# A two-block model kernel: a spectral transform folded in half, and another order of work around the convolution after it

## The chip, the cores and the metric

The kernel runs on one core of a Trainium2 chip (eight cores, two dies of four). The metric is device time in microseconds of one execution, here the median of three. The core's engines work at once and meet through semaphores: TensorE (PE; PEld is its weight load), VectorE (DVE), ScalarE (ACT), GpSimd (POOL), and SyncE (SP), whose queue issues nearly all transfers.

## The reference, cut to what matters

A sequence of 256 rows of 1024 values goes through two blocks. The first has a recurrent mixer and an attention layer. The second begins with the part that is changed:

```
p = rmsnorm(x) @ w_in_ab                      # 1024 -> 512 (a), 512 (v), 512 (gate)
f = real(fft2(a as [256, 4 heads, 128], axes=(time, 128), ortho))
ya = einsum("bshd,hde->bshe", f, fnet_map)    # a 128x128 map per head
u = v * sigmoid(gate)
u = depthwise_conv(u, conv_w, 31 taps) + conv_b
yb = silu(layernorm(u as [4 heads, 128]))
x = x + concat(ya, yb) @ w_out_ab
...
x = x + swiglu_ffn(rmsnorm(x))                # then a pool mixer and a second FFN
```

## The kernel before, in words

**Layout.** Values lie channel by channel on the 128 partitions and the 256 time steps along the free axis, eight tiles of 128 channels.

**Weights.** Large weight matrices come as 1 MB slabs of 128x2048 values. SP loads them into a ring of five buffers (`raw`), in the order of the table `PLAN`. ACT copies each into the first half of one of four buffers `W` (line 635, the high part), and DVE writes what is left, raw minus high, into the second half (line 1030, the low part). A product takes three fast matmuls (lines 1602 to 1604: high by high, high by low, low by high). `stream(MATS[n])` emits the split of all slabs up to n at that place of an engine's program, and `fill(k)` is `stream(MATS[k + 3])`. Where the text says slab n, it is `MATS[n]`.

**Who waits.** Each engine runs its own program in the order in which it is written. PE's results go to eight banks of PSUM. The class `Outputs` gives each result its bank in turn, and before PE writes a bank it waits (`bank_free`) until the result that was there before has been read. `o.n += 4` skips four banks.

**Keys and values (first block, 120 to 165 us).** PE makes eight key tiles k0 to k7, then four value tiles v0 to v3 (128x512 each), then the queries q0 to q7, which need the low parts of their input (DVE, `r<-t,r`). ACT finishes each key with the copy of line 759, and its bank is free after that. Before, v0 takes the bank of k4.

**The spectral part (slabs 24 and 25, then 281 to 294 us).** All of it is plain fp32. Per head h, line 1891 multiplies the a-tile with a table of 128 cosines and 128 sines (`cdsd`, 128x256) for both halves of time; ACT copies and scales the eight results. Lines 1899 and 1900 sum over time with tables in `acc[0]` (128x256 each, 16 matmuls). ACT copies f, line 1906 applies `fnet_map`, ACT makes the high part of that and DVE the low part.

**The convolution of 31 taps.** Channels 0 to 2 run on DVE: `taps` is a list of 93 pairs (channel, tap), three of which (tap 0) ACT does, so DVE has 90 steps of 128x256 (line 1033, `f<-f,vec`). A step adds to its own channel's tile. The last eight of the list belong to channel 2 alone. `pump(n)` emits the next n pairs of the list. Channel 3 runs on PE (line 1913): 31 matmuls with diagonal matrices that ACT makes (`dg`, `diagonals`), eight buffers.

**The layer norm and the output product.** For a channel tile d: `ln_mean` (PE, line 1919), `ln_centre` (DVE), square (ACT), `ln_var` (PE, 1924), root (ACT), `ln_inverse` (DVE, line 1451, `lnr<-lnr`), `ln_row` (PE, line 1667, spreads the inverse over a bank), `ln_scale` (DVE), silu and high part (ACT), `ln_low` (DVE). Channel 3 goes first. PE fills the time between with `mixed(kt, c)`, products with slabs 26 to 29 (`w_out_ab`); `both(kt)` is four of these, twelve matmuls 128x512. kt 0 to 3 take the spectral part, kt 4 to 7 the convolution's. The FFN stages follow and are not touched.

Of the kernel before, what the change touches and what calls it, by code (L numbers as in the profile page):

```python
# [6 lines left out]
P, T, D, KT = 128, 256, 1024, 8  # L7
# [10 lines left out]
def slab_plan():  # L18
# [59 lines left out]
    ("norm_mix_g_2", 16), ("norm_ffn_g_2", 16), ("conv_w_2", 124), ("conv_b_2", 4), ("conv_ln_g_2", 4),  # L78
    ("conv_ln_b_2", 4), ("eps", 2),
]  # L80
# [5 lines left out]
NV = _at  # L86
CSTS = [("ident", 128), ("mask", 384), ("cdsd", 256), ("fmap", 512)]
COFF = {}
# [79 lines left out]
def outputs():  # L168
# [41 lines left out]
    o.n += 1  # L210
    o.n += 4
    for c in range(2):
# [122 lines left out]
def two_block_program(nc, w_d, vec_d, cst_d, dft_d, rcnt_d, row_d, x_d, out_d):  # L335
# [6 lines left out]
    with ctx:  # L342
# [3 lines left out]
        def sem(name):  # L346
            return ctx.enter_context(nc.semaphore(name))
# [3 lines left out]
        with ExitStack() as early:  # L351
# [66 lines left out]
        s_b, s_gpad, s_col, s_gt, s_sg, s_tap0, s_tap, s_a, s_ac, s_f, s_fhi, s_flo = (  # L418
            sem(f"s_{n}") for n in ("b", "gpad", "col", "gt", "sg", "tap0", "tap", "a", "ac", "f", "fhi", "flo"))
        s_dg, s_dgm, s_cv3, s_lnm, s_lnv, s_lnc, s_lnq, s_lnr, s_lni, s_lnb, s_lnn, s_cs2, s_clo = (  # L420
            sem(f"s_{n}") for n in ("dg", "dgm", "cv3", "lnm", "lnv", "lnc", "lnq", "lnr", "lni", "lnb", "lnn", "cs2",
# [16 lines left out]
        F0f = F0[:, 0:2048].rearrange("p (k n) -> p k n", k=8)  # L438
        PADW = T + 30
        G0 = F0[:, 0:4 * PADW].rearrange("p (k n) -> p k n", k=4)  # L440
        Vt = F2[:, :, :].rearrange("p (a b) n -> p a (b n)", a=2)
# [177 lines left out]
        @block.gpsimd  # L619
        def _(e):  # L620
            e.wait_ge(s_mv, 12)
            e.dma_start(acc[0][:, :], dft_d).then_inc(s_dft, 16)
            e.wait_ge(s_flo, 4)
            e.dma_start(rc, rcnt_d).then_inc(s_rc, 16)
            e.dma_start(prow[:, :], row_d[0]).then_inc(s_prow, 16)
            e.wait_ge(s_cv3, 1)
            e.dma_start(frow[:, :], row_d[1]).then_inc(s_frow, 16)

        @block.scalar
        def _(e):  # L630
# [249 lines left out]
            p.wait_ge(s_cst, 16)  # L880
            for c in range(2):
                fill(24 + c)
                for d in (2 * c, 2 * c + 1):
# [3 lines left out]
            for h in range(4):  # L887
                for a in range(2):
                    p.wait_ge(*ended("ac", h, a))
                    copy(AC[:, h, a, :], out_of("ac", h, a), scale=rcol[:, 4 + a:5 + a]).then_inc(s_ac, 1)  # L890
# [24 lines left out]

            diagonals(*range(6, 16))
            fill(25)
            diagonals(*range(16, 31))
# [106 lines left out]
        def _(e):  # L1025
# [417 lines left out]
            fill(25)  # L1443

# [29 lines left out]
            fill(26)  # L1474
            for d in range(3):
# [117 lines left out]
        def _(e):  # L1593
# [291 lines left out]
            for c in range(2):  # L1885
                single(24 + c, run("a", 2 * c, 2 * c + 1), R2, s_rlo, 0)
            for h in range(4):
                for a in range(2):
                    bank_free("ac", h, a)
                    p.wait_ge(s_a, h + 1)  # L1890
                    e.matmul(out_of("ac", h, a), F2[:, h, a * P:(a + 1) * P], C("cdsd"), start=True,  # L1891
                             stop=True).then_inc(s_ps, 1)
            p.wait_ge(s_dft, 16)
            for h in range(4):
                bank_free("f", h)
                out = out_of("f", h)
                for a in range(2):
                    p.wait_ge(s_ac, 2 * h + a + 1)
                    e.matmul(out, AC[:, h, a, 0:P], acc[0][:, a * T:a * T + T], start=a == 0, stop=False)
                    done = e.matmul(out, AC[:, h, a, P:256], acc[0][:, (2 + a) * T:(3 + a) * T], start=False,  # L1900
                                    stop=a == 1)
                done.then_inc(s_ps, 1)
            for h in range(4):
                bank_free("fm", h)
                p.wait_ge(s_f, h + 1)
                e.matmul(out_of("fm", h), C("fmap", h * P, P), F2[:, 4 + h, :], start=True,
                         stop=True).then_inc(s_ps, 1)
# [185 lines left out]
def constants():  # L2093

    out = np.zeros((P, NC), np.float32)

    def put(name, a):
        out[:, COFF[name]:COFF[name] + a.shape[1]] = a

    put("ident", np.eye(P))  # L2100
    diag = np.where(np.arange(P)[None, :] <= np.arange(P)[:, None], 0.0, -1e30)
    put("mask", np.concatenate([diag, np.zeros((P, P)), diag], 1))
    d = np.arange(P)
    ang = 2 * np.pi * ((d[:, None] * d[None, :]) % P) / P
    put("cdsd", np.concatenate([np.cos(ang), np.sin(ang)], 1) / np.sqrt(P))
# [76 lines left out]
```

## Time and profile before

| | before |
|---|---|
| median of 3 runs | 729.29 us (729.09 to 730.04) |
| profiled execution, own time | 732.02 us |
| its span | 730.2 us |
| mean granted TensorE clock | 0.995 |
| PE busy | 98% |
| DVE busy | 69% |
| ACT busy | 54% |
| POOL busy | 0% |

The span runs from the first to the last instruction; the execution's own time also has what lies around it. In the timeline each row has a start, a duration, engine, line, operation, and output<-input with tile numbers left out. A PE duration has the drain in it, so the cost of a matmul in a row of them is the distance from one start to the next. A plain fp32 matmul leaves two records. The granted clock is given as a share of 2.4 GHz: 0.50 is 1.2 GHz.

### The profile page before, as it was taken

Reading aid. Unit: us, or ns where it says so; the run is one execution under the profiler, and the core shown is the slowest. Engines: PE = TensorE matmul, PEld = TensorE weight load, DVE = VectorE, ACT = ScalarE, POOL = GpSimd, SP = SyncE. Lnnn points to the kernel's source line nnn. Section 1 sums busy time; section 2 is a strip of 40 time slices with the busy share of each in tenths; the row PEclk is TensorE's granted clock in tenths of the full one; section 3 lists DMA queues with packets and bytes.
Section 4 is the critical chain, followed back from the end, with each engine's and each line's share of the span. In section 5 each row is a group of like instructions: output and inputs, shape, how many; then the busy total and the mean of one; then the engine's idle time right before and its main releaser. Section 6 shows DMA issues by size and latency. Waiting matters only on the chain.

```text
span 730.2 us, 9502 instructions
## 1 busy us (share of the span) xinstructions
PE 714.9 (98%) x3804; PEld 620.6 (85%) x3804; DVE 502.5 (69%) x801; ACT 394.4 (54%) x610; POOL 2.4 (0%) x8
## 2 busy tenths in 40 slices
PE   7999999999999999999999999999999999999996
PEld 5878889889999999888888888888888888888885
DVE  5689996998977889987744545455686445555544
ACT  3156635964886776768644344443666443344423
POOL 0000000000000000000000000000000000000000
PEclk9999999999999999999999999999999999999998
DMA  8999994799836342433755545554326455455201
GB/s 335 415 423 373 423 401 166 260 376 347 355 117 230 118 173 91 176 139 115 289 183 207 187 173 189 206 180 173 116 116 230 179 201 197 174 182 206 74 1 57
DMA packets 23084, 156.11 MB, mean 214 GB/s; under 512 B 2560, under 2 KB 2816, under 8 KB 5120
## 3 DMA queue, kind: packets, MB, share of 16 engines
q1 hardware_dynamic: 22464, 152.88, 54.6%
q0 software_dynamic: 576, 2.62, 0.9%
q8 instruction: 30, 0.49, 0.3%
q14 instruction: 14, 0.11, 0.0%
HBM read 154.44 MB, written 1.05 MB: 213 GB/s over the span
## 4 chain that ended last, share of the span: by engine, by line
PE 91%; DMA 4%; ACT 2%; DVE 1%; SPq 0%; issue 0%; ACTq 0%
PE pb L1602 24%; PE pb L1604 23%; PE pb L1603 23%; PE pb L1671 10%; DMA raw<-w_dram 4%; PE pb L1913 2%; PE pb L2019 1%; PE pb L2087 1%; PE pb L1941 1%; DVE raw L1033 1%; ACT t L751 1%; ACT w L635 0%; ACT r L748 0%; PE pb L1830 0%; PE pb L1811 0%; PE pb L1891 0%
## 5 line engine op out<-in xcount | busy, mean ns | idle before, releaser
L1030 DVE TENSOR_TENSOR w<-raw,w 128x2048 fp32r<-128x2048 f32 x97 | 221.2, 2289 | 140.7 <-ACT w L635 140.7
L635 ACT ACTIVATE w<-raw 128x2048 fp32r<-128x2048 f32 x97 | 184.8, 1914 | 143.2 <-PE pb L1604 114.7
L1602 PE MATMUL pb<-w,r 128*128 128x512 f32 (+1 forms) x608 | 239.1, 393 | 1.9 <-ACT f L759 1.7
L1604 PE MATMUL pb<-w,r 128*128 128x512 f32 (+1 forms) x608 | 235.5, 387 | 0.0
L1603 PE MATMUL pb<-w,r 128*128 128x512 f32 (+1 forms) x608 | 235.1, 387 | 0.0
L1602 PEld LDWEIGHTS pb<-w,r 128*128 128x128 f32 x608 | 114.2, 188 | 24.8 <-issue 2.1
L1604 PEld LDWEIGHTS pb<-w,r 128*128 128x128 f32 x608 | 114.2, 188 | 23.8
L1603 PEld LDWEIGHTS pb<-w,r 128*128 128x128 f32 x608 | 114.3, 188 | 22.3
L1602 PE MATMUL pb<-r,w 128*128 128x256 f32 x288 | 82.4, 286 | 0.0
L1604 PE MATMUL pb<-r,w 128*128 128x256 f32 x288 | 81.5, 283 | 0.0
L1603 PE MATMUL pb<-r,w 128*128 128x256 f32 x288 | 81.5, 283 | 0.0
L1033 DVE SCALAR_TENSOR_TENSOR raw<-raw,acc 128x1024 f32<-128x1024 f32 x64 | 75.1, 1218 | 6.4 <-DMA raw<-w_dram 6.4
L1671 PE MATMUL pb<-h,ow 128*128 128x256 f32 x256 | 56.8, 381 | 1.9 <-ACT h L696 1.8
L1671 PEld LDWEIGHTS pb<-h,ow 128*128 128x128 f32 x256 | 48.5, 191 | 10.2 <-issue 3.6
L1603 PEld LDWEIGHTS pb<-r,w 128*128 128x128 f32 x288 | 55.2, 192 | 0.1
L1602 PEld LDWEIGHTS pb<-r,w 128*128 128x128 f32 x288 | 55.2, 192 | 0.1
L1604 PEld LDWEIGHTS pb<-r,w 128*128 128x128 f32 x288 | 55.2, 192 | 0.0
L964 ACT ACTIVATE t<-pb,rn 128x256 f32<-128x256 f32 x44 | 20.7, 476 | 59.7 <-PE pb L1604 59.6
L1033 DVE SCALAR_TENSOR_TENSOR f<-f,vec 128x256 f32<-128x256 f32 x114 | 46.6, 472 | 0.2
L1033 DVE SCALAR_TENSOR_TENSOR t<-pb,rn,t 128x256 f32<-128x256 f32 x44 | 21.1, 483 | 22.8 <-ACT t L964 22.8
L1671 PE MATMUL pb<-t,ow 128*128 128x256 f32 x128 | 27.8, 379 | 0.0
L1671 PEld LDWEIGHTS pb<-t,ow 128*128 128x128 f32 x128 | 24.3, 190 | 3.3
(208 smaller groups left out, 663.3 us busy)
## 6 DMA issues: line engine op xcount, KB each, us to landing
raw<-w_dram SPq DMA_DIRECT2D x129, 1024.0 KB, 4.9
ow<-w_dram SPq DMA_DIRECT2D x8, 1024.0 KB, 15.2
ow<-w_dram SPq DMA_DIRECT2D x8, 512.0 KB, 17.1
oh<-w_dram SPq DMA_DIRECT2D x2, 1024.0 KB, 23.6
x<-x_dram SPq DMA_DIRECT2D x2, 512.0 KB, 5.8
f<-rc_dram POOLq DMA_DIRECT2D x1, 1024.0 KB, 5.0
acc<-row_dram POOLq DMA_DIRECT2D x2, 512.0 KB, 6.1
out_dram<-f SPq DMA_DIRECT2D x4, 256.0 KB, 2.3
```

What stands on the lines that cost most here:

```text
L635: return e.activation(out, in_, ACT.Copy, **kw)
L751: e.activation(tt[kt][:, :], F3[:, kt, :], ACT.Identity, **kw).then_inc(done, 1)
L964: e.activation(tt[(at_ - 1) % 4][:, :], bank_of("gu", layer, i, a)[:, 0:T], ACT.Silu, scale=rn[:, 2 * layer, a:a + 1]).then_inc(s_sgt, 1)
L1030: return e.tensor_tensor(out, a, b, op)
L1033: return e.scalar_tensor_tensor(out, a, s, b, op0, op1, **kw)
L1602: e.matmul(out, a_hi, b_hi, start=start, stop=False)
L1603: e.matmul(out, a_hi, b_lo, start=False, stop=False)
L1604: return e.matmul(out, a_lo, b_hi, start=False, stop=stop)
L1671: return e.matmul(out, slab[:, o:o + P], rhs, start=start, stop=stop)
L1913: done = e.matmul(out_of("cv", 3), dg[j % 8], G0[:, 3, j:j + T], start=j == 0, stop=j == 30)
L1941: done = e.transpose(bank_of("tx", n, a, m)[:, j * P:j * P + P], Xt[:, a, o:o + P], ident)
L2019: done = e.transpose(out[:, j * T + a * P:j * T + a * P + P], tt[4 + (at_ - 1) % 4][:, j * P:j * P + P], ident)
```

## The change

1. **Fold over the head dimension.** `cdsd` has 128 columns: 63 sines (rows 1 to 63) and 65 cosines (rows 0 and 64 to 127), since the other frequencies mirror these. Line 1891's eight matmuls become 128 wide, two heads share a bank, and ACT copies four results in place of eight.
2. **Fold over time.** The 16 matmuls of lines 1899 and 1900 compute 130 outputs (`NS`) in place of 256, the two tables into two halves of a bank. ACT gathers each head's f with three copies (64x130, 64x130, 1x130) in place of one.
3. **The map in two halves.** Line 1906 becomes two matmuls per head: 130 columns with the map, and 126 read backwards with a mirrored map. POOL makes the two sets of maps: two more loads of 128 KB behind the load of the time tables, and six operations of 128x256.
4. **Banks.** `o.n += 4` goes, and `ac` takes four banks in place of eight. From the values to the spectral part every result moves by four banks: v0 takes the bank of k1, v1 that of k2, v2 of k3, v3 of k7.
5. **Orders.** On ACT, slab 28 is split after the diagonals, and six diagonals move behind the spectral part. On DVE the taps run as 43, four times 3, 10 and 25, the low parts of slabs 26 and 27 come behind the spectral part's low parts, slabs 28 and 29 behind the taps, and `ln_inverse(3)` behind the last tap. On PE the means of channels 0 and 1 come ahead of `both(2)`.

```diff
-    o.n += 4
...
-    for h in range(4):
-        o.out(("ac", h, 0), ("ac", h, 1))
+    for g in range(2):
+        o.out(("ac", g, 0), ("ac", g, 1))
...
+            e.wait_ge(s_na, 7)
+            for i in range(2):
+                e.dma_start(sqt[i][:, :], dft_d[:, 4 * T + i * T:5 * T + i * T]).then_inc(s_mir, 16)
...
+            for i in range(2):
+                e.tensor_scalar(sqt[i][:, :], sqt[i][:, :], sgn, None, MUL).then_inc(s_fold, 1)
...
+                e.tensor_tensor(part, part, sqt[i][:, :], ADD).then_inc(s_fold, 1)
+            for i in range(2):
+                e.wait_ge(s_fold, 3 + i)
+                e.tensor_scalar(sqt[i][:, :], C("fmap", i * T, T), sgn, None, MUL).then_inc(s_fold, 1)
...
+            stream(MATS[26])
+            spectral(0, 1)
+            stream(MATS[27])
+            diagonals(0, 1, 2)
+            spectral(2, 3)
...
-                copy(F2[:, 4 + h, :], out_of("f", h)).then_inc(s_f, 1)
-                if h < 3:
-                    diagonals(2 * h, 2 * h + 1)
+                cosines, sines = [bank_of("f", h)[:, o_:o_ + NS] for o_ in (0, T)]
+                copy(F2[0:64, 4 + h, 0:NS], sines[0:64, :]).then_inc(s_sin, 1)
+                copy(F2[64:128, 4 + h, 0:NS], cosines[64:128, :])
+                p.wait_ge(s_sin, h + 1)
+                copy(F2[0:1, 4 + h, 0:NS], cosines[0:1, :]).then_inc(s_f, 1)
...
-            pump(36)
-            fill(24)
-            pump(20)
+            pump(46)
             for h in range(4):
                 p.wait_ge(s_fhi, h + 1)
                 low(R1, h, out_of("fm", h), s_flo)
                 pump(3)
-            fill(25)
...
-            pump(3)
+            stream(MATS[27])
+            pump(68 - tap_n["n"])
             ln_centre(3)
-            pump(9)
+            pump(len(taps) - tap_n["n"])
             ln_inverse(3)
-            pump(85 - tap_n["n"])
+            ln_centre(0)
+            ln_centre(1)
             ln_scale(3)
-            pump(4)
+            stream(MATS[28])
             ln_low(3)
-            pump(4)
-            for d in range(3):
-                ln_centre(d)
-            fill(26)
+            ln_centre(2)
+            stream(MATS[29])
...
+                e.matmul(out_of("fm", h)[:, 0:NS], C("fmap", h * P, P), F2[:, 4 + h, 0:NS], start=True, stop=False)
+                e.matmul(out_of("fm", h)[:, NS:T], sqt[h // 2][:, h % 2 * P:h % 2 * P + P], F2[:, 4 + h, T - NS:0:-1], start=False,
                          stop=True).then_inc(s_ps, 1)
...
             both(1)
             ln_row(3)
-            both(2)
             ln_mean(0, (s_tap, tap_at[0, 30]))
             ln_mean(1, (s_tap, tap_at[1, 30]))
+            both(2)
```

DVE from the last low part of the spectral part on (`r<-pb,r`; `w<-raw,w` is a slab's low part, `f<-f,vec` taps, `lnr<-lnr` is `ln_inverse`). Before:

```order
L1030 TENSOR_TENSOR r<-pb,r 128x256
L1033 SCALAR_TENSOR_TENSOR f<-f,vec 128x256 x3
L1030 TENSOR_TENSOR w<-raw,w 128x2048
L1033 SCALAR_TENSOR_TENSOR f<-f,vec 128x256 x3
L1033 SCALAR_TENSOR_TENSOR f<-pb,f 128x256
L1033 SCALAR_TENSOR_TENSOR f<-f,vec 128x256 x9
L1451 RECIPROCAL lnr<-lnr 128x2
L1033 SCALAR_TENSOR_TENSOR f<-f,vec 128x256 x5
L1033 SCALAR_TENSOR_TENSOR f<-f,vec,pb 128x256
```

and of the change:

```order
L1054 TENSOR_TENSOR r<-pb,r 128x256
L1057 SCALAR_TENSOR_TENSOR f<-f,vec 128x256 x3
L1054 TENSOR_TENSOR w<-raw,w 128x2048 x2
L1057 SCALAR_TENSOR_TENSOR f<-f,vec 128x256 x10
L1057 SCALAR_TENSOR_TENSOR f<-pb,f 128x256
L1057 SCALAR_TENSOR_TENSOR f<-f,vec 128x256 x25
L1472 RECIPROCAL lnr<-lnr 128x2
L1057 SCALAR_TENSOR_TENSOR f<-pb,f 128x256 x2
L1057 SCALAR_TENSOR_TENSOR f<-f,vec,pb 128x256
```

Before, 13 taps (5, 4 and 4) come behind the inverse; now all 90 come ahead of it.

PE around `ln_row(3)` (`pb<-cst,lnr`), from the end of `both(1)` on. Before:

```order
L1604 MATMUL pb<-w,r 128x512
L1667 MATMUL pb<-cst,lnr 128x128 x2
L1602 MATMUL pb<-w,r 128x512
L1603 MATMUL pb<-w,r 128x512
L1604 MATMUL pb<-w,r 128x512
```

and of the change:

```order
L1625 MATMUL pb<-w,r 128x512
L1688 MATMUL pb<-cst,lnr 128x128 x2
L1945 MATMUL pb<-f,ones_sb 128x256 x2
L1623 MATMUL pb<-w,r 128x512
L1624 MATMUL pb<-w,r 128x512
```

The two means of channels 0 and 1 (L1945) now stand directly behind the row; the work ahead of the row is the same.

## Rows read from the trace of the kernel before

**Rows 1.** The page, part 4: the chain that ended last, by engine
```profile
PE 91%; DMA 4%; ACT 2%; DVE 1%; SPq 0%; issue 0%; ACTq 0%
```
**Rows 2.** Waits of PE: waiter <- releaser: us in total, times, longest
```profile
PE pb L1692 <- DVE f L1030: 3.9, 1, 3.9
...
PE pb L1602 <- ACT f L759: 1.7, 1, 1.7
```
**Rows 3.** Timeline of PE, spectral part to layer norm (start us, duration us, what)
```profile
281.68 3.62 PE L1891 MATMUL pb<-cst,f 128*128 128x256 f32 x16
285.13 0.59 PE L1899 MATMUL pb<-acc,f 128*128 128x256 f32 x2
...
292.04 1.89 PE L1906 MATMUL pb<-f,cst 128*128 128x256 f32 x8
293.76 13.55 PE L1913 MATMUL pb<-f,acc 128*128 128x256 f32 x62
...
315.29 0.38 PE L1667 MATMUL pb<-cst,lnr 128*128 128x128 f32 x2
...
327.55 0.50 PE L1602 MATMUL pb<-w,r 128*128 128x512 f32 x1 [0.21 <-DVE r L1030]
```
**Rows 4.** Timeline of PE, two scores of the attention: 128 columns, then 256
```profile
187.13 0.39 PE L1810 MATMUL pb<-f 128*128 128x128 f32 x2
187.35 0.60 PE L1811 MATMUL pb<-f 128*128 128x256 f32 x2
```
**Rows 5.** Timeline of DVE, convolution and layer norm
```profile
273.81 13.14 DVE L1033 SCALAR_TENSOR_TENSOR f<-f,vec 128x256 f32<-128x256 f32 x33
286.88 4.47 DVE L1030 TENSOR_TENSOR w<-raw,w 128x2048 fp32r<-128x2048 f32 x2
...
299.20 0.41 DVE L1030 TENSOR_TENSOR r<-pb,r 128x256 fp32r<-128x256 f32 x1
299.53 1.26 DVE L1033 SCALAR_TENSOR_TENSOR f<-f,vec 128x256 f32<-128x256 f32 x3
...
312.90 0.17 DVE L1451 RECIPROCAL lnr<-lnr 128x2 f32<-128x2 f32 x1 [0.26 <-ACT lnr L906]
...
318.40 2.04 DVE L1033 SCALAR_TENSOR_TENSOR f<-f,vec 128x256 f32<-128x256 f32 x4
320.36 1.30 DVE L1033 SCALAR_TENSOR_TENSOR f<-pb,f 128x256 f32<-128x256 f32 x3
```
**Rows 6.** Timeline of ACT: copies of f, a copy of 128x128 among them
```profile
197.44 0.96 ACT L635 ACTIVATE t<-pb 128x256 f32<-128x256 f32 x4
```
**Rows 7.** Windows of one us: busy us of PE, PEld, DVE, ACT, POOL, then granted clock
```profile
13.00:14.00 1.00, 0.88 (x3) 0.81 (x4) 1.00 (x2) 0.17 (x1) 0.00 (x0) 0.59 0.95 393
14.00:15.00 1.00, 1.00 (x4) 0.80 (x3) 0.95 (x6) 0.24 (x2) 0.00 (x0) 0.50 1.05 438
15.00:16.00 1.00, 1.00 (x4) 0.82 (x3) 0.47 (x2) 0.58 (x1) 0.00 (x0) 0.50 1.06 446
16.00:17.00 1.00, 1.00 (x4) 0.79 (x4) 1.00 (x3) 0.00 (x0) 0.00 (x0) 0.71 0.97 406
```
**Rows 8.** Timeline of PE: last key, first value, first query, first weighted sum
```profile
139.57 0.28 PE L1765 MATMUL pb<-r,w 128*128 128x256 f32 x1
141.57 0.47 PE L1602 MATMUL pb<-w,r 128*128 128x512 f32 x1 [1.72 <-ACT f L759]
...
163.44 0.28 PE L1602 MATMUL pb<-r,w 128*128 128x256 f32 x1
...
198.38 0.60 PE L1830 MATMUL pb<-t,f 128*128 128x256 f32 x2
```
**Rows 9.** Timeline of ACT: keys k2 and k4 finished
```profile
139.53 0.51 ACT L759 ACTIVATE f<-f,kb 128x256 f32<-128x256 f32 x1
...
140.91 0.51 ACT L759 ACTIVATE f<-f,kb 128x256 f32<-128x256 f32 x1
```
**Rows 10.** Timeline of DVE: low parts of the queries' input
```profile
162.15 2.09 DVE L1030 TENSOR_TENSOR r<-t,r 128x256 fp32r<-128x256 f32 x6
```
**Rows 11.** Issues of transfers: KB each, us to landing; and when POOL's comes
```profile
acc<-dft_dram POOLq DMA_DIRECT2D x1, 512.0 KB, 8.9
...
POOL acc L622 <- DVE mv L1030: 185.6, 1, 185.6
```

More of the change, by code:

```diff
@@ L621, in _ @@
             e.wait_ge(s_mv, 12)
-            e.dma_start(acc[0][:, :], dft_d).then_inc(s_dft, 16)
+            e.dma_start(acc[0][:, :], dft_d[:, 0:4 * T]).then_inc(s_dft, 16)
+            e.wait_ge(s_na, 7)
+            for i in range(2):
+                e.dma_start(sqt[i][:, :], dft_d[:, 4 * T + i * T:5 * T + i * T]).then_inc(s_mir, 16)
+            sgn = V("sgn", 0)
+            e.wait_ge(s_vec, 16)
+            e.wait_ge(s_mir, 32)
+            for i in range(2):
+                e.tensor_scalar(sqt[i][:, :], sqt[i][:, :], sgn, None, MUL).then_inc(s_fold, 1)
+            e.wait_ge(s_cst, 16)
+            for i in range(2):
+                part = C("fmap", i * T, T)
+                e.wait_ge(s_fold, i + 1)
+                e.tensor_tensor(part, part, sqt[i][:, :], ADD).then_inc(s_fold, 1)
+            for i in range(2):
+                e.wait_ge(s_fold, 3 + i)
+                e.tensor_scalar(sqt[i][:, :], C("fmap", i * T, T), sgn, None, MUL).then_inc(s_fold, 1)
             e.wait_ge(s_flo, 4)
@@ L880, in _, with spectral @@
             p.wait_ge(s_cst, 16)
-            for c in range(2):
-                fill(24 + c)
-                for d in (2 * c, 2 * c + 1):
+            def spectral(*ds):
+                for d in ds:
                     p.wait_ge(*ended("a", d))
                     copy(F2[:, d, :], out_of("a", d)).then_inc(s_a, 1)
+            stream(MATS[26])
[3 more added lines that the diff above has]
+            spectral(2, 3)
             p.wait_ge(s_col, 3)
-            for h in range(4):
+            for g in range(2):
                 for a in range(2):
-                    p.wait_ge(*ended("ac", h, a))
-                    copy(AC[:, h, a, :], out_of("ac", h, a), scale=rcol[:, 4 + a:5 + a]).then_inc(s_ac, 1)
+                    p.wait_ge(*ended("ac", g, a))
+                    copy(AC[:, g, a, :], out_of("ac", g, a), scale=rcol[:, 4 + a:5 + a]).then_inc(s_ac, 1)
             for h in range(4):
                 p.wait_ge(*ended("f", h))
-                copy(F2[:, 4 + h, :], out_of("f", h)).then_inc(s_f, 1)
-                if h < 3:
-                    diagonals(2 * h, 2 * h + 1)
+                cosines, sines = [bank_of("f", h)[:, o_:o_ + NS] for o_ in (0, T)]
[3 more added lines that the diff above has]
+                copy(F2[0:1, 4 + h, 0:NS], cosines[0:1, :]).then_inc(s_f, 1)
             for h in range(4):
@@ L914, in ln_high @@
                 copy(hi_of(R1, 4 + d), tt[4 + d][:, :]).then_inc(s_cs2, 1)
-            diagonals(*range(6, 16))
-            fill(25)
-            diagonals(*range(16, 31))
+            diagonals(*range(3, 31))
+            stream(MATS[28])
             p.wait_ge(*ended("cv", 3))
@@ L1886, in _ @@
                 single(24 + c, run("a", 2 * c, 2 * c + 1), R2, s_rlo, 0)
-            for h in range(4):
+            for g in range(2):
                 for a in range(2):
[L1889 to L1892, printed above, removed]
+                    bank_free("ac", g, a)
+                    for b in range(2):
+                        h = 2 * g + b
+                        p.wait_ge(s_a, h + 1)
+                        done = e.matmul(out_of("ac", g, a)[:, b * P:b * P + P], F2[:, h, a * P:(a + 1) * P], C("cdsd"),
+                                        start=True, stop=True)
+                    done.then_inc(s_ps, 1)
             p.wait_ge(s_dft, 16)
@@ L1895, in _ @@
                 bank_free("f", h)
-                out = out_of("f", h)
                 for a in range(2):
[L1898 to L1901, printed above, removed]
+                    p.wait_ge(s_ac, 2 * (h // 2) + a + 1)
+                    col = AC[:, h // 2, a, h % 2 * P:h % 2 * P + P]
+                    e.matmul(bank_of("f", h)[:, 0:NS], col, acc[0][:, a * T:a * T + NS], start=a == 0, stop=False)
+                    done = e.matmul(bank_of("f", h)[:, T:T + NS], col, acc[0][:, (2 + a) * T:(2 + a) * T + NS],
+                                    start=False, stop=a == 1)
                 done.then_inc(s_ps, 1)
+            p.wait_ge(s_fold, 6)
             for h in range(4):
@@ L2103, in constants @@
     d = np.arange(P)
-    ang = 2 * np.pi * ((d[:, None] * d[None, :]) % P) / P
-    put("cdsd", np.concatenate([np.cos(ang), np.sin(ang)], 1) / np.sqrt(P))
+    row = np.arange(P)
+    freq = np.where(row >= 64, row - 64, np.where(row == 0, 64, row))
+    ang = 2 * np.pi * ((d[:, None] * freq[None, :]) % P) / P
+    put("cdsd", np.where((row >= 64) | (row == 0), np.cos(ang), np.sin(ang)) / np.sqrt(P))
     s = np.arange(T)
@@ L2167 @@
     cst, dft, rc = constants()
-    cst[:, COFF["fmap"]:COFF["fmap"] + 512] = a["fnet_map_2"][0].transpose(1, 0, 2).reshape(P, 512)
+    row = np.arange(P)
+    vec[:, VOFF["sgn"]] = np.where((row >= 64) | (row == 0), 1.0, -1.0)
+    fmap, at = a["fnet_map_2"][0].transpose(1, 0, 2).reshape(P, 512), COFF["fmap"]
+    own = np.where(row >= 64, row - 64, np.where(row == 0, 64, row))
+    cst[:, at:at + 512] = fmap[own]
+    other = np.flatnonzero(row % 64)
+    mirror = np.zeros((P, 2 * T), np.float32)
+    mirror[other] = fmap[P - own[other]]
+    dft = np.concatenate([dft, mirror], 1)
     x = np.ascontiguousarray(a["x"][0].T.reshape(KT, P, T).transpose(1, 0, 2))
```

13 lines of the change are left out of this document (7 added, 6 removed).

## The prediction

> **What bounds the kernel now.** I read the page first. The chain that ended last is 91% PE [rows 1], so a change counts by what it does to PE's program. The list of PE's waits comes next: the long ones are 3.9 us near the start and 1.7 us at the first value, for ACT's work on a key [rows 2]. Then the timeline of PE from the spectral part on: the reader is to see that it runs from 281.68 to 327.55 without a gap, and waits only 0.21 us at the end of the layer norm [rows 3]. PE is the bound there by a hair. The timeline of DVE over the same stretch shows why: it runs taps from 273.81, and its last tap ends at 320.36 [rows 5], while `ln_row(3)` goes at 315.29 on PE [rows 3]. Two engines are full side by side, and the change takes work from one of them.
>
> **Part 1, the folds on PE.** A plain matmul of 256 columns costs 0.43 us: sixteen in 285.13 to 292.04, 6.91 us [rows 3]. One of 128 costs 0.22 us, the distance of two starts in the attention [rows 4]. Line 1891: 281.68 to 285.13, 3.45 us for eight [rows 3]; eight of 128 columns are 1.76: 1.7 us less. Lines 1899 and 1900: 16 of 130 columns are 16 x 0.223 = 3.6, 3.3 us less. Line 1906: four take 292.04 to 293.76, 1.72 us; eight of 130 and 126 columns are 1.76, nothing gained. Reading an operand backwards has no row; I take nothing for it, and twice the price of those four, 0.9 us, as the other end. Sum: 5.0 us less. The convolution's first matmul then goes at 288.7 instead of 293.76.
>
> ACT's gathering: three copies per head. Four copies of heads' tiles, two of 256 and two of 128 columns, take 0.96 us [rows 6], so three small ones are 0.6 to 0.9 us, against PE's 0.89 us per head. They keep pace; the last map may wait 0.3 us. The diagonals that moved have eight buffers. All of this is hidden for another reason, in part 2.
>
> **Part 2, DVE's chain up to `ln_inverse(3)`.** This decides. DVE's start at 273.81 doesn't move by the folds. Ahead of the inverse now stand all 90 taps, four low parts of the spectral part, slabs 26 and 27, and one centring. A tap costs 0.396 us where channels alternate (33 from 273.81 to 286.88) and 0.49 us where one channel follows itself (four from 318.40 to 320.36); eight of the list are of that kind. A low part is 0.33 us (299.20 to 299.53), two slabs 4.47 us, a centring 1.30 / 3 = 0.43 us [all rows 5]. So 82 x 0.396 + 8 x 0.49 + 4 x 0.33 + 4.47 + 0.43 = 32.5 + 3.9 + 1.3 + 4.5 + 0.4 = 42.6 us, and the taps end at 316.4. With the reciprocal's 0.17 us [rows 5] PE can place `ln_row(3)` at 316.6. Before it went at 315.29 [rows 3]: **1.3 us later**.
>
> PE's own work lets it be there at 315.29 - 5.0 = 310.3. It then stands for 6.3 us, since the row is in front of everything else in its queue: the means, `both(2)`, the rest of slabs 26 to 29, then both FFNs. So the whole 5.0 us of part 1 is given back, and 1.3 us more. Behind the row PE has the same matmuls as before (only their order differs). DVE's two slab splits that now lie between the centrings are 2.2 us each, while PE has over 7 us of its own there; I take them as covered. If that cover goes, PE waits 0 to 1 us for the inverses of channels 0 to 2.
>
> Three small things hide in the same 6.3 us: ACT's gathering, backward reading, and the later split of slab 28.
>
> **Part 3, TensorE's clock behind the stall.** The trace shows one gap of this kind: PE idle for 3.9 us up to 11.8 [rows 2], and soon after it the granted clock goes to 0.50 and comes back: 0.59, 0.50, 0.50, 0.71 in four windows [rows 7]. 0.50 is 1.2 GHz, 1 is 2.4. The lost part is 0.41 + 0.50 + 0.50 + 0.29 = 1.7 us of work. The new stall is longer, and PE resumes into its densest stretch. I take 1.7 us. The lower end is 0 (the clock falls and returns while PE stands, or doesn't fall); the upper end 1.5 times as much, 2.6 us, if PE resumes right after a fall and needs longer to get it back.
>
> **Part 4, the banks.** v0 waited for the fifth key, whose last copy on ACT runs from 140.91 to 141.42 [rows 9], and PE started at 141.57 [rows 8]. It now needs the second key only, and v1 the third, ready at 140.04 [rows 9]. PE can start 0.12 us after 139.57 [rows 8], so 1.9 us sooner. But the queries behind the values need DVE's low parts, which start at 162.15 [rows 10], the first ready at 162.6; PE came there at 163.44 [rows 8], so 0.8 us are left. Further on the first weighted sum, at 198.38 [rows 8], needs ACT's copies from 197.44 on, two of four of them, done by 198.0 [rows 6]: 0.4 us are left. I take **0.4 us** less, between 0 and 1.9. DVE follows PE into the convolution (it waits for the gate products), so this part moves parts 2 and 3 as a whole.
>
> **Part 5, POOL.** It starts when the last sum of the first block is done, at 185.6, and the first load lands 8.9 us after its issue [rows 11]; the six operations run at about 195 to 200 us and are needed at about 287. Nothing waits. 128 KB twice more is an eighth of a slab each. I take 0. If they slow DVE's softmax steps at 192 to 198 us one for one, with 0.4 us each as DVE's own steps of that size [rows 5], it is up to 2.4 us.
>
> **Sum.** +1.3 + 1.7 - 0.4 = +2.6 us. Against the profiled execution's own time, 732.02 us (span 730.2), that is 734.6. The median of the runs, 729.29, lies 2.7 us under that execution, and the same difference on it gives **731.9 us**.
>
> **The rivals.**
>
> *The clock doesn't count* (15%). Everything as above without part 3: +0.9 us, 730.2. For it: only one gap in this trace shows a fall, and that was among small matmuls at the start. Against: the new gap is half as long again.
>
> *The banks give more* (8%). If DVE and ACT in the first block follow the earlier PE, up to 1.9 us are gained: 1.3 + 1.7 - 1.9 = +1.1, 730.4. Against: DVE shows no waiting time in that stretch, its steps stand one behind another.
>
> *The folds' gain is kept, faster than before* (8%). One mechanism: DVE reaches `ln_inverse(3)` before PE does. It needs 6.3 us less over its 90 taps, 0.07 each, so a tap at 0.33 us instead of 0.396; from there on PE's 5.0 us count. 0.33 is what a low part costs, so DVE can work at that pace on this size, but none of the taps in the trace does. Time: -5.0 - 0.4 = -5.4 us, 723.9.
>
> *POOL is in DVE's way* (6%). Up to 2.4 us on the softmax steps in part 5, of which PE's slack there takes about 0.5 and the 0.4 us of part 4 go too: +2.6 + 1.9 = +4.5 at the most, half of it likely: 733.0. The Trainium skill, "GPSIMD Engine Reference", section "Specifications", says that GpSimd shares its SBUF interfaces with VectorE and that instructions with two SBUF inputs collide. No row here has POOL computing beside DVE.
>
> *The change doesn't do what it says* has no room: the order of the instructions shows each part.
>
> **How the numbers follow.** The forecast has 63%. A measurement of this kernel tells about 0.2% from no change, 1.46 us. Slower by more: the forecast and POOL's case, 69%. Within: the clock's and the banks' cases, 23%. Faster: 8%. The range takes in the clock's case (730.2) and the banks' (730.4) below. Above, the forecast's unknowns at their ends are 1.3 + 2.6 - 0 = +3.9, 733.2, and POOL's likely case, with a little for a wait in the layer norm. 730.0 to 733.6 leaves out the faster case and the worst of POOL's.
>
> **What the next profile would show.** Lines 1914, 1923 and 1924 of the changed kernel in about 5.3 us where 10.4 were. The first value's wait gone from PE's list, and a new one at the top: PE `pb<-cst,lnr` waiting about 6 us for DVE's reciprocal. DVE without a gap from its first tap to that reciprocal, 42 to 43 us. A granted clock of 0.50 for some 3 us around 313 to 320 us. If PE's wait there is under 2 us, part 2 is wrong; if it is there and the clock stays at 1, part 3 is; if the first query goes more than 1 us sooner, part 4 is.

## The result, and the profile after

The changed kernel takes **733.65 us** (median of six, 733.14 to 734.24) where the kernel before takes 729.45 (six runs beside it): ratio 1.0053, 95% interval 1.0043 to 1.0064, so 4.2 us slower by the medians (3.1 to 4.7 by the interval, whose middle is 3.9). The forecast was 731.9 with a range up to 733.6. The direction is right, the size is some 1.7 us too small, and the value lies at the range's upper end: 0.05 us over it as a time, and just inside it as a difference (4.2 us, where the range goes up to 4.3 over the 729.29 that it was worked out from).

The profiled execution has a time of 733.46 us and a span of 731.7, only 1.5 over the span before. The two executions differ in their first 140 us, where the code is the same: the last key runs at 136.78 instead of 139.57 [rows 8]. I therefore compare distances. From VectorE's first tap to the end it is 731.7 - 271.42 = 460.28 us where it was 730.2 - 273.81 = 456.39: **+3.89 us**, nearly all of what the medians show.

The chain by engine on the page of the changed kernel, beside [rows 1]; DVE has come into it:

```profile
PE 81%; DVE 15%; ACT 2%; DMA 2%; issue 0%; SPq 0%; DVEq 0%
```

PE's waits in the changed kernel (waiter, releaser, us in total, times, longest), beside [rows 2]. The first line is new and the largest; the wait of the first value for ACT is gone:

```profile
PE pb L1688 <- DVE lnr L1472: 6.2, 1, 6.2
PE pb L1713 <- DVE f L1054: 3.5, 1, 3.5
...
PE pb L1623 <- DVE r L1054: 1.2, 2, 1.0
```

PE's timeline in the changed kernel, beside [rows 3]: L1914, 1923/1924 and 1931/1932 are the folded transform and maps, L1939 the convolution, L1688 `ln_row(3)`, the last row the first product of `both(4)`.

```profile
279.28 1.95 PE L1914 MATMUL pb<-cst,f 128*128 128x128 f32 x16
281.07 0.39 PE L1923 MATMUL pb<-acc,f 128*128 128x130 f32 x2
...
284.64 0.39 PE L1931 MATMUL pb<-f,cst 128*128 128x130 f32 x2
...
286.43 13.55 PE L1939 MATMUL pb<-f,acc 128*128 128x256 f32 x62
...
314.32 0.69 PE L1688 MATMUL pb<-cst,lnr 128*128 128x128 f32 x2 [6.21 <-DVE lnr L1472]
...
329.02 0.51 PE L1623 MATMUL pb<-w,r 128*128 128x512 f32 x1 [0.19 <-DVE r L1054]
```

From 279.28 to 286.43 it is 7.15 us, where it was 12.08: 4.93 less. Then PE stands for 6.21. And from `ln_row(3)` to `both(4)` it takes 14.70 us, where it took 12.26. VectorE in the same stretch, beside [rows 5]:

```profile
271.42 17.10 DVE L1057 SCALAR_TENSOR_TENSOR f<-f,vec 128x256 f32<-128x256 f32 x43
...
294.51 4.49 DVE L1054 TENSOR_TENSOR w<-raw,w 128x2048 fp32r<-128x2048 f32 x2
...
303.21 10.98 DVE L1057 SCALAR_TENSOR_TENSOR f<-f,vec 128x256 f32<-128x256 f32 x25
314.11 0.16 DVE L1472 RECIPROCAL lnr<-lnr 128x2 f32<-128x2 f32 x1
```

No gap: 42.69 us of steps up to the reciprocal. The windows of the changed kernel (columns as in [rows 7], here of two us) show the granted clock, the third column from the end:

```profile
311.00:313.00 2.00, 0.00 (x0) 0.00 (x0) 1.86 (x5) 0.00 (x0) 0.00 (x0) 0.94 0.00 0
313.00:315.00 2.00, 0.68 (x3) 0.68 (x4) 1.19 (x4) 0.00 (x0) 0.00 (x0) 0.50 0.00 0
315.00:317.00 2.00, 2.00 (x7) 1.54 (x6) 0.67 (x2) 0.00 (x0) 0.00 (x0) 0.50 0.00 0
317.00:319.00 2.00, 2.00 (x6) 1.59 (x5) 2.00 (x3) 1.37 (x4) 0.00 (x0) 0.50 0.00 0
319.00:321.00 2.00, 2.00 (x9) 1.56 (x8) 1.10 (x2) 0.17 (x1) 0.00 (x0) 0.85 0.23 33
```

The clock fell while PE stood, and stayed at 1.2 GHz until about 320. It wasn't this execution alone: the mean granted clock is 0.988 to 0.991 in all six executions of the changed kernel, and 0.992 to 0.999 in those of the kernel before that were timed beside the experiments (one slow one among them, 1212.88 us at 0.557, is left out of every ratio).

| stretch | before | after | difference |
|---|---|---|---|
| last key to first query | 23.87 | 23.16 | -0.71 |
| last key to first tap | 134.24 | 134.64 | +0.40 |
| first tap to `ln_row(3)` | 41.48 | 42.90 | +1.42 |
| `ln_row(3)` to `both(4)` | 12.26 | 14.70 | +2.44 |
| `both(4)` to the end | 402.65 | 402.68 | +0.03 |

The stretches are in us, from the start of one row to the start of the next.

The theory that goes into the experiments: the stall is VectorE's lengthened chain, and the clock's fall behind it costs 2.4 us. The rivals: the new order on PE costs the 2.44; POOL's work eats the banks' gain (the +0.40).

### The profile page after: what moved, and what is told of

It is laid out like the page before. It is cut to its first block, busy times and chain, and to the rows that moved or that the text cites. A ratio compares the mean times of both kernels' runs of the same rounds, so it can differ in the third digit from the quotient of the medians.

```text
span 731.7 us, 9534 instructions
## 1 busy us (share of the span) xinstructions
PE 712.4 (97%) x3812; PEld 618.7 (85%) x3812; DVE 502.8 (69%) x801; ACT 393.1 (54%) x614; POOL 10.5 (1%) x16
## 3 DMA queue, kind: packets, MB, share of 16 engines
HBM read 154.64 MB, written 1.05 MB: 213 GB/s over the span
## 4 chain that ended last, share of the span: by engine, by line
PE 81%; DVE 15%; ACT 2%; DMA 2%; issue 0%; SPq 0%; DVEq 0%
PE pb L1623 20%; PE pb L1625 20%; PE pb L1624 20%; PE pb L1692 13%; DVE f L1057 5%; DVE w L1054 4%; DVE raw L1057 3%; PE pb L2045 1%; DMA raw<-w_dram 1%; DVE f L1054 1%; PE pb L2113 1%; DVE r L1054 1%; PE pb L1967 1%; DMA x<-x_dram 1%; PE pb L1784 0%; PE pb L1785 0%
```

## The experiments

Each experiment was timed against the kernel before on the same chip. "Tap to end" is the span less the start of VectorE's first tap, of the profiled execution, against 456.39 of the kernel before.

| kernel | median us | before us | ratio, 95% interval | tap to end |
|---|---|---|---|---|
| changed kernel | 733.65 | 729.45 | 1.0053 (1.0043 to 1.0064) | +3.89 |
| e1_orders | 736.15 | 729.86 | 1.0087 (1.0073 to 1.0101) | +6.24 |
| e2_warm | 731.76 | 729.86 | 1.0028 (1.0015 to 1.0040) | +1.35 |
| e3_folds | 729.53 | 729.86 | 0.9997 (0.9989 to 1.0006) | -1.08 |
| e4_banks | 730.64 | 729.86 | 1.0014 (1.0005 to 1.0022) | +0.89 |
| e4b_banks | 730.13 | 729.93 | 1.0000 (0.9991 to 1.0008) | +0.03 |
| e5_late | 733.63 | 729.93 | 1.0050 (1.0038 to 1.0062) | +3.44 |
| e6_tuned | 729.54 | 729.93 | 0.9993 (0.9984 to 1.0002) | -0.28 |
| e8_inverse | 729.76 | 729.93 | 0.9996 (0.9987 to 1.0005) | +0.54 |
| e9_warm_tuned | 728.54 | 729.64 | 0.9984 (0.9975 to 0.9993) | -1.87 |
| e10_slab29_last | 729.29 | 729.64 | 0.9995 (0.9986 to 1.0005) | -0.84 |

### Filling the stall: e2_warm

```diff
             both(1)
+            bank_free("ln", 0)
+            for _ in range(14):
+                e.matmul(PB[6][:, 0:T], ones, C("fmap", 0, T), start=True, stop=True)
             ln_row(3)
```

> The changed kernel with 14 matmuls of 256 columns, whose product nobody reads, between both(1) and ln_row(3): at 0.43 us each they fill 6.0 of the 6.2 us that PE stood. Theory (the low clock behind the stall costs 2.4 us): the clock stays at 1.00 through the layer norm, from ln_row(3) to both(4) it takes 12.3 us where the change takes 14.70, and the median is 2.0 to 2.6 us below the changed kernel, about 731.2. Rival (the clock's fall costs little, the 2.4 us are the new order of PE and late inverses): the clock stays up and the time falls by under 0.8 us. Rival (the clock falls for another reason than idleness): 0.50 is still there and nothing is gained.

PE's rows for `ln_row(3)` and `both(4)` in e2_warm, then its windows over them:

```profile
315.37 0.43 PE L1688 MATMUL pb<-cst,lnr 128*128 128x128 f32 x2 [0.16 <-DVE lnr L1472]
...
327.57 0.50 PE L1623 MATMUL pb<-w,r 128*128 128x512 f32 x1 [0.19 <-DVE r L1054]
```

```profile
315.00:317.00 2.00, 1.84 (x10) 1.45 (x10) 1.03 (x4) 0.00 (x0) 0.00 (x0) 1.00 0.00 0
317.00:319.00 2.00, 2.00 (x10) 1.65 (x9) 2.00 (x3) 1.42 (x4) 0.00 (x0) 1.00 0.00 0
```

12.20 us instead of 14.70, at a clock of 1.00. VectorE's 42.91 from first tap to row are the same as in the change. So the new order on PE costs nothing by itself, and the 2.44 are the clock, shown by giving PE work that nobody reads. The median fell by 1.9 us, the distance from tap to end by 2.5; the median's fall is 0.1 short of the 2.0 that the theory asked for at least. The mean granted clock is 0.993 to 0.997 in its six executions. The theory holds, and both rivals fall. What is left over the kernel before, 1.35 us from tap to end, is the row that comes 1.43 us later by VectorE's chain.

### The orders without the folds: e1_orders

```diff
-            pump(36)
-            fill(24)
-            pump(20)
+            pump(46)
...
             ln_row(3)
-            both(2)
             ln_mean(0, (s_tap, tap_at[0, 30]))
             ln_mean(1, (s_tap, tap_at[1, 30]))
+            both(2)
```

(and the change's order of slabs 26 to 29, centrings and taps on VectorE, as in the diff of the change; ScalarE keeps the order of before).

> The kernel before with the change's new orders on VectorE and TensorE around the layer norm alone: no folds, no moved banks, no POOL products. Theory (the stall is as long as PE is early; the clock falls only behind a long one): VectorE's chain is 1.3 us longer and PE arrives where it did, so ln_row(3) waits 1 to 1.6 us, the clock stays at 1.00, and the median is 1.0 to 1.8 us over the kernel before. Rival (the new order itself costs more than its 1.3 us, by inverses of the other channels that come late, or PE's mixed order): 3 us or more over. Rival (any stall at this place brings the clock down): 0.50 shows in the windows behind the row, and it is 2.5 to 4 us over.

It is 6.3 us slower, 4.5 over the theory's upper end. The first rival's "3 us or more" came in, but neither of the mechanisms that it named did; 0.50 shows, as in the second rival (319 to 321 us), which put the size too low. VectorE's timeline, three rows, then PE's row in e1_orders:

```profile
291.54 0.42 DVE L1030 TENSOR_TENSOR r<-pb,r 128x256 fp32r<-128x256 f32 x1 [2.17 <-ACT r L635]
...
307.12 0.42 DVE L1033 SCALAR_TENSOR_TENSOR f<-pb,f 128x256 f32<-128x256 f32 x1 [1.05 <-PE pb L1916]
...
318.35 0.16 DVE L1448 RECIPROCAL lnr<-lnr 128x2 f32<-128x2 f32 x1
```

```profile
318.56 0.69 PE L1664 MATMUL pb<-cst,lnr 128*128 128x128 f32 x2 [4.67 <-DVE lnr L1448]
```

With the unfolded transform VectorE comes to the first low part of the spectral part, and to the first centring, before their inputs are there: it stands 2.17 and 1.05 us, 3.2 in all. The tap-to-row distance is 46.29, not 42.90. I had counted VectorE's steps and forgotten that its new order needs PE's results sooner. So the folds are not worthless in the change: they hide these 3.2 us. The stall of 4.67 is enough for the clock too: `ln_row(3)` to `both(4)` takes 332.19 - 318.56 = 13.63, 1.4 over the 12.20 of e2_warm and over the 12.26 of the kernel before.

### The folds without the orders: e3_folds

The edit is the reverse of the one above, on the changed kernel: its folds, banks and POOL work, with the orders of before on VectorE and TensorE. ScalarE keeps the order of the change.

> The changed kernel (folds, banks, POOL's products) with the orders of the kernel before on VectorE and TensorE around the layer norm. Theory: VectorE's chain up to the reciprocal of channel 3 is the old one, so PE's 5 us less turn into waits for VectorE: about 2.8 us at ln_row(3) and more at the means and before both(4). The clock stays at 1.00 or nearly. The median is within 1 us of the kernel before (-0.8 to +0.5). Rival (a stall of some 3 us is enough for the clock to fall): 1.5 to 3 us over before. Rival (the folds' gain is kept): 3 us or more below before.

PE's waits from 300 us to `both(4)` in e3_folds:

```profile
302.48 0.63 PE L1980 MATMUL pb<-cst,x 128*128 128x128 f32 x4 [0.42 <-DVE r L1054]
303.91 0.66 PE L1980 MATMUL pb<-cst,x 128*128 128x128 f32 x4 [0.80 <-DVE r L1054]
309.26 0.61 PE L1953 MATMUL pb<-ones_sb,t 128*128 128x1 f32 x4 [0.64 <-ACT t L927]
319.06 0.70 PE L1948 MATMUL pb<-f,ones_sb 128*128 128x256 f32 x2 [1.12 <-DVE f L1057]
```

PE waits in pieces of up to 1.1 us, at the low parts, the variance and a mean, and not at `ln_row(3)`: not where I said, but 3.0 us in all. The clock stays at 1.00, and the median is that of the kernel before (729.53 against 729.86). The folds give about 1.1 us from tap to end with the old order. The other 3.9 of the 4.93 go at these four places: the waits are 3.0, and measured from start to start PE's work there takes 3.7 us longer than in the kernel before. VectorE is as full as before: it is busy for 43.06 of the 45 us from 281 on, where it was 42.90 of 45.8.

### The banks alone: e4_banks, e4b_banks

```diff
     o.n += 1
-    o.n += 4
     for c in range(2):
         o.out(("v", 2 * c), ("v", 2 * c + 1))
...
+    o.n += 4
     for h in range(4):
         o.out(("ac", h, 0), ("ac", h, 1))
```

> The kernel before with the values' outputs on the other banks alone, as in the change; all the rest as before. Theory A (POOL's two loads and six operations take back the banks' gain in the changed kernel): from the last key to the first tap it takes 0.4 to 0.8 us less than before, and the median is that much lower. Theory B (the banks' gain is lost for itself, as the rest of the first block is bound by VectorE's and ScalarE's steps): same distances as before behind the first query, median within 0.2 us.

That was e4_banks. It had the added line of the diff one stage earlier, ahead of the "a" outputs, and made a wait of its own: 0.61 us of PE for VectorE at 131.9 us behind the last key. The distance to the first tap was 134.75, and the kernel was 0.8 us slower than before, so it tells little of the banks. The cleaner one is e4b_banks, whose diff is the one above:

> The kernel before with the values' outputs on the other banks, and from there on every bank number as in the changed kernel up to the spectral part (the first try put the old numbers back one stage earlier, and PE waited 0.61 us there for a bank). Theory now (the banks' 0.7 us at the first query are given back before the first tap, because ScalarE's splits of slabs 12 to 14 wait for slabs that land no sooner): the first query goes 0.7 us nearer to the last key, the first tap does not (134.2 to 134.8 us behind it), and the median is within 0.3 us of the kernel before. Rival (POOL's loads and operations took back the gain): the first tap is 0.4 us or more nearer and the median 0.4 to 0.8 us below.

The first query goes 23.16 us behind the last key, as in the change, and the median is that of before. What sets the start of the softmax steps is a row of VectorE, its pair of slab splits ahead of them. Here in the kernel before, then in e4b_banks and in the changed kernel:

```profile
185.67 4.49 DVE L1030 TENSOR_TENSOR w<-raw,w 128x2048 fp32r<-128x2048 f32 x2
```

```profile
183.70 4.49 DVE L1030 TENSOR_TENSOR w<-raw,w 128x2048 fp32r<-128x2048 f32 x2
```

```profile
182.90 4.49 DVE L1054 TENSOR_TENSOR w<-raw,w 128x2048 fp32r<-128x2048 f32 x2
```

The last key is at 139.57, 137.58 and 136.78, so this pair starts 46.10, 46.12 and 46.12 us behind it. VectorE doesn't move when PE gains 0.7 us: they are given back as waits. And slab 14's landing, to which ScalarE's 1.7 us wait pointed in the changed kernel, is no cause: e4b_banks has a wait of 1.27 there without POOL's loads, e1_orders has none, and neither is faster.

### POOL later: e5_late

```diff
+            e.wait_ge(s_olo, 8)
             e.wait_ge(s_na, 7)
             for i in range(2):
                 e.dma_start(sqt[i][:, :], ...
```

> The changed kernel with POOL's two extra loads and its six operations put behind the output product of the attention (about 222 us instead of 184 us), where ScalarE and VectorE have slack. Theory (POOL costs nothing): as the changed kernel within 0.3 us. Rival (the loads delay slab 14, and POOL slows VectorE's softmax steps): ScalarE's 1.7 us wait for slab 14 is gone and the median is 0.4 to 0.8 us below the changed kernel.

733.63, the changed kernel's time. ScalarE's wait for slab 14 is still 1.25 us, so the loads never made it. From last key to first tap it is 134.41. All profiled executions of this study lie between 134.2 and 134.8, with and without banks or POOL. The kernel before, at 134.24, is at the low end; e1_orders has the same code up to there and takes 134.68. So the +0.40 in the table above is within this spread, and no cost of the change. The two medians, 733.65 and 733.63, show no price of POOL; one of a few tenths they could not show.

### The inverse sooner: e8_inverse

```diff
-            pump(len(taps) - tap_n["n"])
+            pump(8)
             ln_inverse(3)
+            pump(len(taps) - tap_n["n"])
```

> The changed kernel with one line of VectorE's order moved: ln_inverse(3) comes after 8 of the last 22 taps instead of after all. Theory: the reciprocal is ready 14 taps (5.5 to 6.2 us) sooner, so PE waits under 1 us at ln_row(3), and then stands some 2 us at the first mean, which needs the last tap of channel 0, and less at the others. The clock stays at 1.00, both(4) goes 2 to 4.5 us sooner than in the changed kernel: median 729.2 to 731.7. Rival (the stall only moves whole to the means, with the clock's fall behind it): within 0.7 us of the changed kernel.

One line gives back 3.9 us of median (729.76), and the rival, that the stall moves whole to the means, falls. The three waits that PE has now, in its timeline of e8_inverse:

```profile
310.30 1.13 PE L1946 MATMUL pb<-f,ones_sb 128*128 128x256 f32 x4 [1.00 <-DVE f L1057]
...
317.61 1.05 PE L1951 MATMUL pb<-ones_sb,t 128*128 128x1 f32 x8 [0.26 <-ACT t L927]
319.63 1.02 PE L1951 MATMUL pb<-ones_sb,t 128*128 128x1 f32 x4 [0.97 <-ACT t L927]
```

One part was wrong: the clock still fell, to 0.60 from 319, 0.50 from 321 to 325 and 0.69 after, though no wait was over 1.0 us. In the last two of the rows PE had only six matmuls of one column beside its waits.

### Another order: e6_tuned, and the same with its short waits filled: e9_warm_tuned

```diff
             ln_centre(3)
-            pump(len(taps) - tap_n["n"])
+            pump(8)
             ln_inverse(3)
-            ln_centre(0)
-            ln_centre(1)
+            pump(5)
             ln_scale(3)
-            stream(MATS[28])
+            pump(4)
             ln_low(3)
+            pump(2)
+            ln_centre(0)
+            ln_centre(1)
+            pump(6)
             ln_centre(2)
-            stream(MATS[29])
+            stream(MATS[28])
             for d in range(3):
                 ln_inverse(d)
+            stream(MATS[29])
```

(on PE `both(2)` comes right behind `ln_row(3)`, `both(3)` ahead of the third mean).

> The changed kernel with other orders of the same work: VectorE takes the inverse of channel 3 after 76 taps instead of 90, scales and splits it before the last taps, and slab 29 comes behind the other inverses; PE takes both(2) right behind ln_row(3), and whole groups between the means. Theory (the change's gain on PE is lost only because VectorE's chain to that inverse is long): the inverse comes some 6 us sooner, PE waits under 1 us at ln_row(3), no 0.50 in the clock, and both(4) goes 2 to 3.5 us sooner than before: median 726 to 728. Rival (VectorE is full from the first tap to the layer norm's end, so any order only moves the waits): the waits come back at the means and at both(4), and the median is that of the kernel before within 1 us.

It ends at the time of before: the median is 1.5 us over what the theory allowed, and within the 1 us of the rival. The row goes at 308.64 without a stall, 36.55 us behind the first tap, and then three short waits follow. They are shown with the windows around them, in e6_tuned:

```profile
316.17 0.70 PE L1949 MATMUL pb<-f,ones_sb 128*128 128x256 f32 x2 [0.75 <-DVE f L1057]
316.71 0.95 PE L1954 MATMUL pb<-ones_sb,t 128*128 128x1 f32 x8
317.84 0.71 PE L1954 MATMUL pb<-ones_sb,t 128*128 128x1 f32 x4 [0.18 <-ACT t L927]
319.59 0.80 PE L1627 MATMUL pb<-w,r 128*128 128x512 f32 x1 [1.04 <-DVE w L1054]
```

```profile
315.00:317.00 2.00, 1.25 (x8) 0.78 (x6) 1.14 (x4) 0.00 (x0) 0.00 (x0) 1.00 0.00 0
317.00:319.00 2.00, 1.37 (x10) 1.20 (x10) 2.00 (x2) 1.62 (x2) 0.00 (x0) 0.80 0.00 0
319.00:321.00 2.00, 1.41 (x3) 1.16 (x4) 2.00 (x5) 1.94 (x5) 0.00 (x0) 0.50 0.31 41
321.00:323.00 2.00, 2.00 (x8) 1.57 (x7) 1.07 (x2) 0.00 (x0) 0.00 (x0) 0.50 0.83 344
323.00:325.00 2.00, 2.00 (x8) 1.71 (x7) 1.74 (x4) 1.44 (x4) 0.00 (x0) 0.50 1.02 397
```

PE stood 1.97 us in all, and the clock was at 1.2 GHz for some six (0.50 in three windows, and 0.80 in the one ahead). The waits aren't all that is thin there: between 315.4 and 319.6 us PE did no more than one matmul of 256 columns and six of one column. The fall was expected by neither theory, and the next kernel, e9_warm_tuned, asks whether the clock counts here:

```diff
             both(3)
+            bank_free("ln", 2)
+            idle(4, 2)
             ln_mean(2, (s_tap, tap_at[2, 30]))
             for d in range(3):
                 ln_var(d)
+            p.wait_ge(s_clo, 1)
+            idle(5, 3)
             mixed(7, 0, 0, 1)
```

(`idle(bank, n)` is n of the matmuls of e2_warm.)

> The kernel with the retuned orders (e6_tuned) and, in its three short waits, five matmuls of 256 columns whose product nobody reads: two before the mean of channel 2, three before the first product with slab 28 (0.43 us each, 2.2 us where PE waits 1.97). In e6_tuned the granted clock was 0.50 for some 6 us behind these three waits. Theory (short waits near each other bring the clock down too, and that took back what the order gained): the clock stays at 1.00, from the first tap to the first turn after the layer norm it takes 58 to 59.3 us where e6_tuned takes 60.40 and the kernel before 60.72; median 727.3 to 728.5. Rival (VectorE's chain sets the end of the layer norm there, the clock only hid in its slack): within 0.5 us of e6_tuned. Rival (the clock falls for another reason): 0.50 is still there.

The clock is 1.00 in every window from 313 to 329, for instance

```profile
319.00:321.00 2.00, 2.00 (x13) 1.54 (x12) 2.00 (x5) 1.53 (x3) 0.00 (x0) 1.00 0.51 66
```

and the first turn after the layer norm is here in e6_tuned, then in e9_warm_tuned:

```profile
332.49 1.03 PE L1971 MATMUL pb<-cst,x 128*128 128x128 f32 x8
```

```profile
330.46 1.03 PE L1971 MATMUL pb<-cst,x 128*128 128x128 f32 x8
```

From the first tap it is 330.46 - 271.68 = 58.78 us, 1.6 less than e6_tuned's 332.49 - 272.09 = 60.40. The median is 728.54, **faster than the kernel before by 1.1 us**, 0.5 to 1.8 by the ratio's interval: the one version here that beats both kernels clear of the noise. How much of this the five matmuls bought is less sure. In the two traces it is 1.6 us; the medians, each against the kernel before beside it, differ by 0.7 (-0.4 and -1.1), and their intervals overlap. The mean granted clock of the executions points the same way: 0.988 to 0.995 in e6_tuned, 0.993 to 0.997 here.

### Slab 29 behind the low parts: e10_slab29_last

```diff
             for d in range(3):
                 ln_inverse(d)
-            stream(MATS[29])
             for d in range(3):
                 ln_scale(d)
             for d in range(3):
                 ln_low(d)
+            stream(MATS[29])
```

(PE: rows, all products with slab 28, then those with slab 29; four idle matmuls instead of three.)

> As e9_warm_tuned, with VectorE's split of slab 29 (2.2 us) put behind the three scalings and low parts instead of before them, and TensorE's order fitted to that: the rows first, then all products with slab 28, then those with slab 29. Theory: the low parts come 1.5 to 2 us sooner, PE waits 0.2 to 0.8 us for slab 29 in their place, and the end is within 0.5 us of e9_warm_tuned, since the sum of VectorE's work is the same: median 727 to 728.5. Rival (PE is released by the low parts alone): 1 us or more below e9_warm_tuned.

729.29: the median misses the expectation by 0.8 and lies over e9_warm_tuned. PE's wait for slab 29 is as small as expected (0.2 us), but there is one idle matmul more (0.43), and a wait of 0.4 us in its own issue is in its list:

```profile
PE pb L1627 <- issue: 0.4, 1, 0.4
```

`both(4)` does go sooner, 50.43 us behind the first tap where e9_warm_tuned has 51.85, but the first turn goes 59.23 behind it, 0.45 later. So the low parts coming sooner gained nothing. The extra matmul and the wait behind the turn would make up the 0.8, which I didn't test.

## Why the prediction came out as it did

**Part 1, the folds on PE: right.** 5.0 us said, 4.93 measured. Reading backwards costs nothing: eight matmuls of 130 and 126 columns take 1.79 us (284.64 to 286.43), as priced. ScalarE's gathering never showed: PE has no gap from 279.28 to 286.43.

**Part 2, VectorE's chain: right.** A stall of 6.3 said, 6.21 measured; the row 1.3 later said, 1.42 measured against the first tap. What I left out there is that VectorE's new order runs only because the folds make its inputs early; e1_orders shows 3.2 us of waits without them. In the change itself that term is zero, so the sum was right without it, but I hadn't seen why.

**Part 3, the clock: right mechanism, a term too small.** I took 1.7 us from the fall near the start [rows 7]; it is 2.44, by e2_warm 2.50. This is the larger part of the miss. The two falls differ in how long PE stood, 3.9 and 6.21 us, and in how long the low clock lasted once PE was back. At the start the rows sum up to 1.7 us of lost clock. Here 0.50 holds from PE's return at 314.3 to some 320; why it lasts longer here, no run shows. The upper end of 2.6 held it. The case "the clock doesn't count" (15%) falls. The Trainium skill's rule that I set against the sum ("TensorE: Matmul & The Clock Gate", section "HAM oscillation", that long idle gaps of TensorE put it back to half rate, each time) agrees with the trace: 6.21 us of idleness, 0.50.

**Part 4, the banks: a wrong step.** I let 0.4 us of the 0.7 survive, because ScalarE's copies for the first weighted sum seemed to leave that much room. But those copies sit behind softmax steps that go through VectorE, and VectorE's position doesn't move: its pair of splits starts 46.1 us behind the last key with old and new banks. I had written, against the rival of a larger gain, that VectorE's steps stand one behind another there, and didn't apply it to my own 0.4. (Nor was that quite so: VectorE waits 1.16 and 0.56 us for ScalarE at 170 us in the kernel before, and just as long in e4b_banks.) The banks are worth nothing that shows: e4b_banks has a ratio of 1.0000, whose interval of 0.6 us to either side would not exclude 0.4 by itself, but the pair of splits didn't move by 0.1.

**Part 5, POOL: right**, nothing by e5_late. The rival "POOL is in DVE's way", whose 733.0 is nearest to the result, is no explanation of it. Its figure doesn't follow from its terms either: half of 1.9 us more than +2.6 is 732.8. But there was more to the mechanism than the result tells: POOL's steps did meet VectorE's (last section), and it was nearly always POOL that was slower.

**The sum.** 1.3 + 1.7 - 0.4 became 1.42 + 2.44 + 0 = 3.9. The medians say 4.2, with an interval of 3.1 to 4.7. The clock (0.7), the banks (0.4) and 0.1 of part 2 explain the 1.3 that lie between +2.6 and +3.9. The remaining 0.3 are within the noise. The two misses add up and don't cancel, and both lie about where the prediction had put its upper end (2.6 for the clock, 0 for the banks): so the total landed at the edge of the range.

## What to carry to other kernels

When two engines are full side by side, time taken off one is mostly lost unless the other's chain gets shorter too (e3_folds kept 1.1 of 4.9 us); follow the releasing engine's steps to the wait first. Here a wait of TensorE cost more than its length where it was long (4.67 and 6.21 us), and where short ones lay close together among very small matmuls, since the clock fell behind them. Where such a wait can't be removed, matmuls without use that fill it can pay: 2.5 us in the trace (1.9 of median) for a 6.2 us stall, and 1.6 us in the trace (0.7 of median, within the noise) for three waits of 2 us in all.

## What the runs showed of the hardware that I had not expected

**Short waits can bring the clock down.** Three waits of 0.75, 0.18 and 1.04 us within 4.2 us were followed by six us at 0.50 (e6_tuned); with them filled the clock stayed at 1.00. Between them PE ran one matmul of 256 columns and six of one column. These small ones alone didn't do it: the kernel before has six of one column in a row at 322.41, and e9_warm_tuned has them too, both at 1.00. Whether the waits alone would have, without them, no run shows. In e8_inverse two waits of 0.26 and 0.97 us among the same six were enough, and e3_folds had four waits of 0.42 to 1.12 us spread over 17 us, with dense products between, and the clock stayed at 1.00. The Trainium skill, "TensorE: Matmul & The Clock Gate", section "A second HAM failure mode: psum-queue depth-cycling", says that small pauses between groups of matmuls can make the clock oscillate; e6_tuned agrees, with waits for VectorE and ScalarE.

**The clock's price by gap:** 1.4 us behind 4.67 us, 2.4 to 2.5 behind 6.21, 1.6 behind the three short ones. By these traces the last is two thirds of the price of a stall three times as long; the medians show less (0.7).

**POOL's steps vary twofold.** Of the same two operations on 128x256, the scaling took 0.97 us each in the changed kernel and 2.07 in e5_late, the addition 1.62 and 0.72. These two rows are of the changed kernel, the two of the second fence of e5_late:

```profile
194.43 1.93 POOL L632 TENSOR_SCALAR sq<-sq,vec 128x256 f32<-128x256 f32 x2 [9.40 <-DMA sq<-dft_dram]
196.34 3.24 POOL L637 TENSOR_TENSOR cst<-cst,sq 128x256 f32<-128x256 f32 x2
```

```profile
226.62 4.14 POOL L633 TENSOR_SCALAR sq<-sq,vec 128x256 f32<-128x256 f32 x2 [1.95 <-DMA sq<-dft_dram]
230.74 1.43 POOL L638 TENSOR_TENSOR cst<-cst,sq 128x256 f32<-128x256 f32 x2
```

In each, the slow pair ran while VectorE was in the subtraction of a slab, an operation with two SBUF inputs (195.98 to 198.26 in the changed kernel, 224.65 to 229.15 in e5_late). The other six traces with these steps show the same: the pair that overlaps the subtraction takes 3.2 to 4.1 us, and it is the scaling in five of them and the addition in e2_warm. Without an overlap the two take 1.9 and 1.4 us. That fits contention between the two engines, but spans of POOL are rough and no run was made for it, so the cause stays open.
